# Token-major projections in pairs of weight chunks, with one gather slot given up for a weight buffer

## What is computed

```python
mod = (silu(c) @ w_ada + b_ada)                       # shift, scale, gate, twice
h = rmsnorm(x, g1) * (1 + scale1) + shift1
proj = h @ w_in                                       # q, k, v, u, gv, gate_a, gate_b: 7 x 1024 columns
out_b = stick_breaking_attention(q, k, v)             # 8 heads x 128
gv = layernorm(gelu(proj_gv)); out_a = gelu(proj_u) * (tril(w_s) @ gv + b_s)
merged = sigmoid(gate_a) * (out_a @ w_ba) + sigmoid(gate_b) * (out_b @ w_bb)
x = x + gate1 * (merged @ w_out)
h2 = rmsnorm(x, g2) * (1 + scale2) + shift2
s = (h2 @ w_query) @ sub_keys.T                       # 8 heads, two times 128 key scores
experts, gates = top16(top16(s_0) + top16(s_1))       # 16 of 16384 experts per head and token
act = gelu(h2 . expert_down[experts])                 # one row of 1024 each
x = x + gate2 * sum(gates * act * expert_up[experts])
```

## Time and profile before

| | us |
|---|---|
| median of 3 runs | 2341.11 (2339.73 to 2342.93) |
| the profiled execution | 2341.77 |
| its span, first to last instruction | 2340.0 |
| PE, DVE busy | 1712.1 (73%), 1630.5 (70%) |
| DMA moved | 841.14 MB, mean 359 GB/s |

### The profile page before, as it was taken

One profiled execution on the slowest core, in us unless ns is written; L12 is line 12 of the kernel. 1 busy time (PEld: TensorE's weight loads), 2 busy tenths in 40 slices (PEclk: granted clock), 3 DMA queues, 4 the chain that ended last, 5 costly groups with the idle time before them and its releaser, 6 DMA issues.

```text
span 2340.0 us, 22796 instructions
## 1 busy us (share of the span) xinstructions
PE 1712.1 (73%) x7010; PEld 1189.8 (51%) x7010; DVE 1630.5 (70%) x3454; ACT 802.8 (34%) x2085; POOL 814.7 (35%) x647
## 2 busy tenths in 40 slices
PE   6998957988889666878777763766460677777776
PEld 2747956845778555644475752765450222222111
DVE  1011168748898878877985968888989866766764
ACT  1121013386345123238413213452122334443332
POOL 0000024324343324434433423443345444444432
PEclk9999978978989787987655586888685899999989
DMA  7786879977989979997896998999999999999997
GB/s 232 277 259 228 299 305 422 421 299 286 410 343 421 393 283 422 418 421 272 345 417 261 412 365 328 375 420 369 363 412 354 390 420 420 421 415 416 378 387 300
DMA packets 129310, 841.14 MB, mean 359 GB/s; under 512 B 15487, under 2 KB 20863, under 8 KB 33882
## 3 DMA queue, kind: packets, MB, share of 16 engines
q0 software_dynamic: 86512, 615.29, 65.3%
q1 hardware_dynamic: 37348, 217.83, 24.8%
q10 hardware_dynamic: 5328, 6.56, 0.8%
HBM read 824.39 MB, written 15.22 MB: 359 GB/s over the span
## 4 chain that ended last, share of the span: by engine, by line
DMA 28%; PE 27%; DVE 22%; ACT 8%; issue 7%; DVEq 5%; ACTq 1%; POOL 1%; SPq 0%; POOLq 0%
DMA gather_ring<-in_experts,expert_numbers 27%; PE bank L749 10%; PE bank L740 8%; DVE gather_ring L1575 7%; DVE expert_sums L1588 7%; PE bank L763 4%; PE bank L1003 3%; ACT L1234 1%; ACT L1091 1%; POOL gather_ring L672 1%; ACT expert_coefs L1238 1%; ACTq L1088 1%; DVEq L1538 1%; DVEq L1551 1%; ACT expert_acts L1234 1%
## 5 line engine op out<-in xcount | busy, mean ns | idle before, releaser
L672 POOL DMA_INDIRECT gather_ring<-in_experts,expert_numbers x576 | 781.0, 1356 | 1486.1 <-DVE expert_sums L1588 810.8
L1588 DVE SCALAR_TENSOR_TENSOR expert_sums<-gather_ring,expert_coefs,expert_sums 128x1024 f32<-128x1024 f32 x378 | 483.3, 1279 | 98.1 <-ACT expert_coefs L1238 96.3
L1575 DVE CUSTOM_DVE_ANT_0 gather_ring<-gather_ring,h_kept 128x1024 f32<-128x1024 f32 x384 | 468.4, 1220 | 90.7 <-DMA gather_ring<-in_experts,expert_numbers 89.7
L1003 PE MATMUL bank<-gather_ring,expert_sums 128*128 128x512 f32 (+1 forms) x768 | 386.3, 641 | 187.6 <-ACT expert_sums L1252 187.3
L1234 ACT ACTIVATE expert_acts<-expert_dots 128x1 f32<-128x1 f32 x576 | 116.4, 202 | 1026.7 <-DVE expert_dots L1575 1023.5
L749 PE MATMUL bank<-hT,weight_chunks 128*128 128x128 f32 (+2 forms) x2304 | 419.7, 345 | 56.5 <-ACT sigmoids L1164 18.1
L749 PEld LDWEIGHTS bank<-hT,weight_chunks 128*128 128x128 f32 x2304 | 384.6, 204 | 87.2 <-ACT qT L1142 14.5
L1003 PEld LDWEIGHTS bank<-gather_ring,expert_sums 128*128 128x128 f32 (+1 forms) x768 | 127.3, 181 | 446.2 <-ACT expert_sums L1252 240.6
L1575 DVE CUSTOM_DVE_ANT_0 gather_ring<-gather_ring,u_and_gv 128x1024 f32<-128x1024 f32 x192 | 234.3, 1223 | 147.7 <-DMA gather_ring<-in_experts,expert_numbers 147.3
L740 PE MATMUL bank<-weight_chunks,hT 128*128 128x256 f32 (+1 forms) x960 | 229.2, 401 | 23.8 <-ACT u_and_gv L1147 10.6
L740 PEld LDWEIGHTS bank<-weight_chunks,hT 128*128 128x128 f32 (+1 forms) x960 | 181.2, 191 | 68.5 <-issue 29.3
(11 more groups left out here) (206 smaller groups left out, 1753.5 us busy)
## 6 DMA issues: line engine op xcount, KB each, us to landing
weight_chunks<-in_w_in SPq DMA_DIRECT2D x84, 1024.0 KB
weight_chunks<-in_w_ada SPq DMA_DIRECT2D x24, 1024.0 KB
weight_chunks<-in_w_query SPq DMA_DIRECT2D x24, 1024.0 KB
weight_chunks<-in_w_branch_a SPq DMA_DIRECT2D x12, 1024.0 KB
weight_chunks<-in_w_branch_b SPq DMA_DIRECT2D x12, 1024.0 KB
weight_chunks<-in_w_out SPq DMA_DIRECT2D x12, 1024.0 KB
gather_ring<-in_experts,expert_numbers POOLq DMA_INDIRECT x576
u_and_gv<-in_cache_k SPq DMA_DIRECT2D x16, 512.0 KB, 10.9
```

Source lines behind the costliest of these rows:

```text
L672: pool.indirect_dma_start(out=ring[:, item % RING, :], out_offset=None, in_=experts, in_offset=bass.IndirectOffsetOnAxis(ap=expert[:, seq( ...
L1003: mm = nc.tensor.matmul(bank[b + half][0:n, :], by[:, r % KEPT, :], up[:, half * 512:(half + 1) * 512], start=(k == 0), stop=(k == TOPK * ...
L1575: nc.vector.tensor_tensor_reduce(out=down, in0=down, in1=h2_of(t), scale=1.0, scalar=0.0, op0=ALU.mult, op1=ALU.add, accum_out=dots[:, c:c ...
L1588: nc.vector.scalar_tensor_tensor(out=a, in0=up, scalar=coef[:, c:c + 1], in1=a, op0=ALU.mult, op1=ALU.add).then_inc(s_vsum, 1)
```

## The change

k, v, gv and out take two weight chunks at once: one matmul streams 2 x 256 columns out of two neighbouring buffers into a whole bank, so a phase has half as many fills. There are four weight buffers (two pairs), and for the room the gather ring has six slots. The clock's assumed times for these phases go from 4.4 us (k) and 3.9 us (v, gv, out) for each 256-column fill to 6.5 and 6.0 us for each 512-column fill. Each half of the keys is now transposed after a pair of v chunks. The sum of four partial sums in the layer norm becomes a sum of two.

```diff
-RING = 7
+RING = 6
-WBUF = 3
+WBUF = 4
+WIDE = 2 * WC
...
+    def phase_wide(self, key, g, chunks, fills):
+        self.fills[key, g], self.chunks[key, g] = self.fill, len(self.last)
+        for _ in range(chunks // 2):
+            self.fill += fills
+            self.last += [self.fill - 1] * 2
...
-        for phase, count, each in (("norm1", 2 * n, 2.0), ("q", 8, 3.9), ("k", 4 * n, 4.4), ("v", 4 * n, 3.9)):
+        for phase, count, each in (("norm1", 2 * n, 2.0), ("q", 8, 3.9), ("k", 2 * n, 6.5), ("v", 2 * n, 6.0)):
...
-        for phase, count, each in (("u", range(8), 3.9), ("gv", range(4 * n), 3.9), ("merge", range(2), 3.9),
-                                   ("gate", range(2 * n), 4.0), ("merge", range(2, 32), 3.9), ("out", range(4 * n), 3.9),
+        for phase, count, each in (("u", range(8), 3.9), ("gv", range(2 * n), 6.0), ("merge", range(2), 3.9),
+                                   ("gate", range(2 * n), 4.0), ("merge", range(2, 32), 3.9), ("out", range(2 * n), 6.0),
...
             def token_major(n, f, src):
-                w = weight(n)
+                weight(n)
+                weight(n + 1)
+                w = wbuf[:, n % WBUF:n % WBUF + 2]
                 out = take(f)
                 for k in range(KC):
-                    mm = nc.tensor.matmul(out[0:src.shape[2], 0:WC], src[:, k, :], w[:, k, :],
+                    mm = nc.tensor.matmul(out[0:src.shape[2], :].rearrange("p (c n) -> p c n", c=2), src[:, k, :], w[:, :, k, :],
                                           start=(k == 0), stop=(k == KC - 1))
...
-                for c in range(4):
+                for c in range(2):
                     for i, t in enumerate(tiles):
-                        token_major(chunk_base(g, "k") + c, fill_base(g, "k") + c * T + i, h[:, :, i * P:i * P + rows_of(t)])
-                    if c == 2:
-                        turn_keys(0)
-                for c in range(4):
+                        token_major(chunk_base(g, "k") + 2 * c, fill_base(g, "k") + c * T + i, h[:, :, i * P:i * P + rows_of(t)])
+                for c in range(2):
                     for i, t in enumerate(tiles):
-                        token_major(chunk_base(g, "v") + c, fill_base(g, "v") + c * T + i, h[:, :, i * P:i * P + rows_of(t)])
-                    if c == 0:
-                        turn_keys(1)
+                        token_major(chunk_base(g, "v") + 2 * c, fill_base(g, "v") + c * T + i, h[:, :, i * P:i * P + rows_of(t)])
+                    turn_keys(c)
...
-                        part = junk[:, (f % 2) * 512:(f % 2) * 512 + WC]
+                        part = junk[:, (f % 2) * WIDE:(f % 2 + 1) * WIDE]
...
-                        nc.vector.tensor_tensor(part, read(f)[:, 0:WC], gate[:, cols], ALU.mult)
+                        nc.vector.tensor_tensor(part, read(f)[:, :], gate[:, cols], ALU.mult)
```

More of the change, by code:

```diff
@@ L114, in __init__ @@
             self.phase("u", g, 4, 2)
-            self.phase("gv", g, 4, n)
+            self.phase_wide("gv", g, 4, n)
             self.phase("merge", g, 16, 2)
-            self.phase("out", g, 4, n)
+            self.phase_wide("out", g, 4, n)
             self.phase("query", g, 8, 2)
@@ L590, in _ @@
                 load_phase(g, "query", "query", 0, range(3))
-                evacuated(sp, fill_base(g, "out") + 4 * T)
+                evacuated(sp, fill_base(g, "out") + 2 * T)
                 for i, t in enumerate(tiles):
@@ L810, in turn_keys @@
                 def turn_keys(half):
-                    evacuated(pe, fill_base(g, "k") + 2 * (half + 1) * T)
+                    evacuated(pe, fill_base(g, "k") + (half + 1) * T)
                     for i, t in enumerate(tiles):
@@ L933, in _ @@
                     channel_major(chunk_base(g, "u") + c, fill_base(g, "u") + 2 * c, h, N)
-                for c in range(4):
+                for c in range(2):
                     for i, t in enumerate(tiles):
-                        token_major(chunk_base(g, "gv") + c, fill_base(g, "gv") + c * T + i, h[:, :, i * P:i * P + rows_of(t)])
+                        token_major(chunk_base(g, "gv") + 2 * c, fill_base(g, "gv") + c * T + i, h[:, :, i * P:i * P + rows_of(t)])
                 n, f = chunk_base(g, "merge"), fill_base(g, "merge")
@@ L964, in _ @@
                 m = mT(g)
-                for c in range(4):
+                for c in range(2):
                     for i in range(T):
-                        token_major(chunk_base(g, "out") + c, fill_base(g, "out") + c * T + i, m[:, :, i * P:(i + 1) * P])
+                        token_major(chunk_base(g, "out") + 2 * c, fill_base(g, "out") + c * T + i, m[:, :, i * P:(i + 1) * P])
                 for i, t in enumerate(tiles):
@@ L1066, in front @@
                         r = rows_of(t)
-                        nc.scalar.copy(gvt(i)[0:r, c * WC:(c + 1) * WC], read(f)[0:r, 0:WC]).then_inc(s_free[f % 4], 1)
-                    if c == 2:
-                        keys_turned(0)
-                for c in range(4):
+                        nc.scalar.copy(gvt(i)[0:r, c * WIDE:(c + 1) * WIDE], read(f)[0:r, :]).then_inc(s_free[f % 4], 1)
+                for c in range(2):
                     for i, t in enumerate(tiles):
@@ L1074, in front @@
                         r = rows_of(t)
[L1075 to L1077 removed]
+                        nc.scalar.copy(values_of(t)[0:r, c * WIDE:(c + 1) * WIDE], read(f)[0:r, :]).then_inc(s_free[f % 4], 1)
+                    keys_turned(c)
                 def logs(n):
@@ L1152, in front @@
                         r = rows_of(t)
-                        nc.scalar.activation(gvt(i)[0:r, c * WC:(c + 1) * WC], read(f)[0:r, 0:WC], ACT.Gelu,
+                        nc.scalar.activation(gvt(i)[0:r, c * WIDE:(c + 1) * WIDE], read(f)[0:r, :], ACT.Gelu,
                                              accum_out=st[0:r, 8 * i + c:8 * i + c + 1]).then_inc(s_free[f % 4], 1)
@@ L1413, in front @@
                     dve.drain()
-                    nc.vector.tensor_reduce(st[0:r, 8 * i + 6:8 * i + 7], st[0:r, 8 * i:8 * i + 4], AX.X, ALU.add)
+                    nc.vector.tensor_tensor(st[0:r, 8 * i + 6:8 * i + 7], st[0:r, 8 * i:8 * i + 1], st[0:r, 8 * i + 1:8 * i + 2], ALU.add)
                     dve.drain()
@@ L1487, in front @@
                 for i, t in enumerate(tiles):
-                    yield CLOCK["out", g, 4 * T - 1] + 1.0 + 4.0 * i
+                    yield CLOCK["out", g, 2 * T - 1] + 1.0 + 4.0 * i
                     kind = "s" if t == SAMPLE else "p"
```

23 lines of the change are left out of this document (10 added, 13 removed).

## The result

The change takes 2414.26 us (median of 4, 2411.50 to 2416.91) where the kernel before, timed beside it, takes 2342.02 (median of 4): ratio 1.0308, 95% interval 1.0294 to 1.0321, 72 us slower. The profiled execution of the change has a span of 2409.9 us. The forecast was 2387, its range 2340 to 2430.

The account below looks back on a forecast made before the run. It took PE to bound A and B, rows on DVE and DMA to bound C, and DMA to bound D. Terms -4 + 27 + 1.5 + 5 + 16 = +45.5 on 2341.8 gave 2387 us, range 2340 to 2430.

Parts of the forecast that it names:

- Width, 0: Matmuls on PE: 512 columns cost twice the time of 256, so the width itself is worth 0.
- rival of cheaper columns: Wide matmuls cost less for a column, so PE leaves B's stretches to the DMA: 2368 us, or 2365; chance 0.07.
- rival in which the rows set the pace: Rows, not PE, pace the touched stretches, so each row that leaves takes its time along: 2332 to 2338 us; chance 0.11.
- A, -4: Stage A: with four buffers the first two gv chunks are called for earlier, saving 2.0 + 1.8 us.
- B's query pieces, +27: Stage B: 13 query pieces instead of 6 ahead of tile 0's end, 7 x 3.9 us; bounds +25 and +32.
- Key transposes, +1.5: Stage B: the second half's key transposes stand directly ahead of attention, ACT copies and hand-overs bare: +1.5 us (0 to 4).
- C's clock, +5: Stage C: 10.3 rows move from front stretches to the free end: +5 us (0 to +12).
- Six slots, +16: Smaller gather ring: +6 us for D's 192 rows and +10 in B and C, about a ninth of DVE's gather waits.
- second rival: The ring becomes the bound: gathers do not shrink with fewer under way, +79 us in D, 2460 in all; chance 0.08.
- third rival: Wide matmuls are cheaper for a column: 2368 us, or 2365 with out's +4 in C gone; chance 0.07.
- well over 100 us: Sign that the prediction is wrong: in C, DVE waits for gathers well over 100 us.
- a query piece that finds its fill ready: Sign that the prediction is wrong: a query piece need not wait for PE; it expected all 13 behind such a wait.

Follow-up runs that it names:

- e12: The change with seven slots (room from two laid-over scratch tensors) and the old clock's length, pairs and four buffers kept: 2346.6 us, ratio 1.0016.
- e4: The kernel before with six gather slots and four weight buffers, clock and width as before: 2373.6 us, ratio 1.0118.
- e2: The kernel before with the shortened clock alone (k 3.25, v, gv and out 3.0 us for a 256-column fill): 2373.6 us, ratio 1.0134.
- e3: The kernel before with six gather slots alone: 2375.6 us, ratio 1.0144.
- e7: The kernel before with five gather slots: 2456.2 us, ratio 1.0476.
- e11: The kernel before with eight gather slots and its three weight buffers, room from two scratch tensors laid over others: 2323.8 us, ratio 0.9916.
- e5: All of the change but the width: 256-column matmuls with shortened clock, six slots and four weight buffers: 2405.1 us, ratio 1.0272.
- e6: The kernel before with the shortened clock and the clock's price of a row lowered (3.76 and 2.88 us instead of 4.0 and 3.0): 2351.7 us, ratio 1.0030.
- e14: The kernel before with the shortened clock for the front of stage C alone (group 2), group 1 as before: 2342.4 us, ratio 0.9997.

## Why the prediction was right, and too low

The sign, the stage and the main mechanism were right; the sum was 27 us short (45.5 against 72). By its steps:

- **Width, 0.** Right: 0.432 us for 512 columns, 55.3 against 55.7 us for k and v, and with the other costs taken away 1.0016 (e12). The rival of cheaper columns is out. The rival in which the rows set the pace is out for B, where the stretches are as long with fewer rows; in C it holds for k and v, as the prediction's own step for C had it.
- **A, -4.** Not there: +0.9 in the change, +2.1 with the fourth buffer but the old clock and width (e4), all within what A varies over the runs. The 3.8 us were largely one execution's: with three buffers gv waits 1.1 to 1.2 us and takes 14.1 in e2, e3, e7 and e11, not 2.0 and 15.8. With four (e4, e5) the wait is gone, but the first gather does not come earlier.
- **B's query pieces, +27.** Right: +28 in the change, +30 alone (e2), 0 when six pieces are put back under the shortened clock (e6).
- **B's gate and the wait ahead of out, not in the sum.** This is the step that failed in B: the working said that k, v, gv and out "take as long as now", which they do, and put nothing for the stretches between them. The gate and the last piece of merge met other rows and other parts of the choice: 16 us in the change, 12 in e6, 7 by the clock alone (e2), 8 by the six slots alone (e3, whose query pieces start at 835.8). The prediction's upper bound of +32 "if the norm ahead of them starts later too" has the direction, not the size. That the choice's parts do it is read from DVE's timeline; no run moves them alone.
- **B's end, not in the sum either.** 7 us in the change and in e5, where late query pieces and six slots meet.
- **Key transposes, +1.5.** No run separates it; attention starts 2.3 us later in the change (468.0 against 465.7 us), no more than in runs without pairs (468.7 in e5).
- **C's clock, +5.** Was 0 (e14). The two sides were larger than the sum had them: in e14 the start of k and the start of out of group 2 lie 627 us apart instead of 652, and from there to D's first row it takes 249 us instead of 225.
- **Six slots, +16.** Measured 33 (e3). D's +6 was right (+5.0, and D took 517 us, inside the 510 to 520 named). The term for B and C was mis-sized: +10, "about a ninth of the waits", where DVE waited 31 us more and the stages grew by 26. The argument, that the ring's size decides nothing where the DMA is full, nearly held for k and v of group 2. But the 0.93 in the earlier trace rows is a mean, and 14 us were lost between attention and gv, at 0.87. The second rival, in which a gather's time does not shrink, is out: with five slots D grew by 30 us, not 165.

Put together: clock 31 and slots 33 make 64; 63 were measured with both (e5). The 9 us between e5 and the change stay open: with the clock of before and seven slots the pairs cost some 3 (1 to 7, e12), and the two were not timed side by side. That 2414 lies just inside the sum's own range of 2360 to 2415 is luck: two of B's terms were missing, and the bounds as given do not add up to that range (with the slots' upper bound, the second rival's 79 us, its top is far higher). In the third rival 2368 less 4 is 2364, not 2365.

What told wrongly was one of the signs that the prediction named, DVE's waits for gathers "well over 100 us" in C as a mark of a costly ring. They stayed at 90.6 us over B and C although the ring cost its full price, since the clock had taken nearly as much of this wait away. Another, "a query piece that finds its fill ready", came true for two of 13, but by late rows, not by a faster PE.

## What to carry to other kernels

A table of assumed times that only sets the order of work is part of the kernel: shorten an entry only by what the engine has been seen to gain, or the work behind it moves to a place where somebody waits for it. A buffer given up for another is to be priced by taking away one, and then a second: here a third weight buffer (with its early call) was worth far more than the eighth gather slot, and the fourth far less than the seventh slot. And an unchanged wait in a profile does not show that its cause costs nothing, if something else has made the waiting engine late.

## What was not expected of the hardware

- A stage gains by one more slot even where the DMA looks full: with a mean share of 0.92 to 0.94, C still moved 364, 372 and 378 GB/s with six, seven and eight slots.
- With five slots D kept a pace of 2.8 us a row ((2454.5 - 1913.3) / 192), against 2.66 with seven ((2340.0 - 1829.1) / 192): taking away two of seven slots cost 6% there. A gather gets shorter when fewer are under way: issue to landing in D took 8.4 us in the median with five slots, 10.3 with six and 15.3 with eight (the trace gives no median for seven). With five, then with eight:

```profile
gather_ring<-in_experts,expert_numbers POOLq DMA_INDIRECT x189, 8.4
...
gather_ring<-in_experts,expert_numbers POOLq DMA_INDIRECT x185, 15.3
```
